# Splitting each early half gate around the values of an attention group, in a decoder step on one core

## The chip, the core and the metric

The kernel runs on one core of a Trainium2 chip. The metric is the device time of one execution in microseconds (us), and lower is better. In this text PE is the engine for matrix products (TensorE), DVE the vector engine, ACT the scalar engine, POOL the GpSimd engine, and SP the engine that issues most of the DMA transfers. PSUM is the memory that PE writes its products to, in eight banks.

## The reference

One layer of a decoder is computed for 512 prompt tokens and 8 sample tokens (520 together, D = 1024). Cut to what matters here:

```python
z = x @ w_in            # q 16x64 | k 4x64 | v 4x64 | pooling 512 | memory query 4x64 | 3 gates x 1024
o_a = sliding-window attention with sinks (window 128, blocks of 128, 16 heads)
o_b = multi-scale causal pooling, mixed and scaled
o_c = cross attention, 4 heads, 256 memory tokens
m = sigmoid(gate_0) * (o_a @ wa) + sigmoid(gate_1) * (o_b @ wb) + sigmoid(gate_2) * (o_c @ wc)
h = layer_norm(ALPHA * x + m @ w_out)
out = layer_norm(ALPHA * h + top-2 mixture of 16 SwiGLU experts(h))
```

All is float32. Products are made in float32 quality from reduced operands: each matrix is split into a high and a low part, and three products are added (high by high, low by high, high by low).

## The kernel before

There are stages on the core, one after the other: the input is transposed and projected; the keys, values and memory keys are made; then 20 attention groups run; then the branches are merged with their gates, projected and normed; and the experts come last.

The change lies in the 20 attention groups. Groups 0 to 15 are window attention ("swa": a block of 128 queries and four heads), groups 16 to 19 are memory attention. The sample tokens' own attention is cut into small steps, and one step, `sample(g)`, stands in each group. On PE a group is: transposes of the normalised probabilities (8 of them, 4 in a "narrow" group 0, 1, 8 or 9, which has one block of keys), scores of the group two ahead, values (probabilities by values), the sample step, and a "fill".

A fill is one half gate: 24 products of 260 columns that have nothing to do with the attention, for a half (260 of the 520 tokens) of one column tile of the gate weights. Fill m is half `m % 2` of gate tile `m // 2`; fills 0 to 15 are the early ones (`EARLY` = 16). Fill 0 stands ahead of the groups, group g has fill g + 1 for g up to 14, group 15 has none, and groups 16 to 19 have fills 16 to 19 with other weights. The products accumulate in PSUM bank 6, and the one after the 24th is told to ACT by `prod_ps`.

A fill waits for two things, and the engines take their instructions in the order in which they are written:

- `gate_out`: ACT has copied the half gate before it out of bank 6 (`filled`, line 790);
- `lo_split`: DVE has made the low part `flo` of the tile's weights (`gate_split`, line 1900, one subtraction of 128x1024), for which ACT first makes the high part `fhi` (line 777). A tile lasts for two fills, so a new one is needed for fills 2, 4, ..., 14, that is in groups 1, 3, ..., 13.

On DVE a group g is, in this order: the copy `pt` of half of the transposes (line 1923 or 1925), the inverse of the sums of group g + 1 (1812, 1815), a piece of the sample step, the four scaled and masked score tiles of group g + 2 (`scaled`, line 1785), the new `flo` when g is odd and under 15, the norms of the sample step, the row maximum of group g + 2 (1798, 1800), and `oalo`, the low part of the group's output (1824). On ACT it is: the exponentials of group g + 1 (695), the copy `pt` of the other half of the transposes (805), the half gate (790), `fhi` when g is odd, and `oahi` (813), the high part of the output, which waits for the values.

The fill is written after the sample step, and its waits stand at its head:

```python
last.then_inc(o_ps, 1)
sample(g)
if fill_after(g) is not None:
    fill(fill_after(g))
```

After the last early fill (`prod_ps` = 16) SP loads the first weights of the merge into the place of the gate weights, and everything later in the kernel follows on that.

Of the kernel before, what the change touches and what calls it, by code (L numbers as in the profile page):

```python
# [16 lines left out]
KD = D // P  # L17
# [40 lines left out]
def decoder_step(nc, a, o):  # L58

    ctx = ExitStack()  # L60
    with ctx:
        def sem(name):
            return ctx.enter_context(nc.semaphore(name))
# [96 lines left out]
        def rt(name, k, shape, dt=F32):  # L160
# [111 lines left out]
        prod_ps, gate_out, m_step, m_val, m_hi, m_lo = (sem(n) for n in (  # L272
            "prod_ps", "gate_out", "m_step", "m_val", "m_hi", "m_lo"))
# [36 lines left out]
        def narrow(g):  # L310

            return groups[g][0] == "swa" and groups[g][1] == 0

        def act_copies(g):

            return sum(not narrow(n) for n in range(g))
# [16 lines left out]
        EARLY = 2 * KD  # L333
        FILLS = EARLY + 4

        def fill_after(g):

            return g + 1 if g < EARLY - 1 else g if g >= EARLY else None
# [34 lines left out]
        def quarter(t, u):  # L373

            return ps[:, 4 + (2 * t + u) % 4, :].rearrange("p (k c) -> p k c", k=4)
# [673 lines left out]
        def _(pe):  # L1049
# [5 lines left out]
            for t in range(NB):  # L1055
                pe.wait_ge(x_in[t], 32 if t == NB - 1 else 16)
                for u in range(2):
# [3 lines left out]
                    for k in range(4):  # L1061
                        last = pe.transpose(quarter(t, u)[:, k, :], xtok[:, t, (4 * u + k) * P:(4 * u + k) * P + P], ident)
                    last.then_inc(xt_ps, 1)
            for k in range(KD):
                last = pe.transpose(ps[:, 3, k * NS:k * NS + NS], xsam[:, k * P:k * P + P], ident[0:NS, 0:NS])
# [15 lines left out]
            def cols(w, n):  # L1081

                return w[:, n * P:n * P + P]
# [7 lines left out]
            def xk(t, k):  # L1091
                return by_half(t[:, k * T:k * T + T])
# [20 lines left out]
            for g in range(4):  # L1113
                last = pe.transpose(ps[:, 7, g * n:g * n + n], pstate[:, g * P:g * P + P], ident[0:n, 0:n])
# [7 lines left out]
            for g in range(4):  # L1122
                for u in range(4):
                    last = pe.transpose(ps[:, 4 + g, u * P:u * P + P],
                                        mtok[:, u % 2, (2 * g + u // 2) * P:(2 * g + u // 2) * P + P], ident)
# [3 lines left out]
            for g in range(4):  # L1129
# [6 lines left out]
                for h in range(2):  # L1136
                    last = pe.matmul(ps[:, 2 * (g % 2) + h, 0:TH], wmix[:, g, :],
                                     pooled[:, g, h * TH:h * TH + TH], start=True, stop=True)
# [19 lines left out]
            for b in range(NB + 1):  # L1158
                out = ps[:, 4 + b // 2, (b % 2) * 256:(b % 2) * 256 + 256]
                last = product([out], [(xhi[:, k * T + b * P:k * T + b * P + P], xlo[:, k * T + b * P:k * T + b * P + P],  # L1160
                                        [whi[0][:, k * 256:k * 256 + 256]], [wlo[0][:, k * 256:k * 256 + 256]])
                                       for k in range(KD)])
# [8 lines left out]
            for p in range(2):  # L1171
                last = pe.transpose(ps[:, 6, p * P:p * P + P], z[:, ZK + p, SEQ - P:SEQ], ident)
            last.then_inc(row_ps, 1)
            for p in range(2):
                last = pe.transpose(ps[0:NS, 6, 256 + p * P:256 + p * P + P], z[:, ZK + p, SEQ:T], ident)
            last.then_inc(row_ps, 1)

            for g in range(4):
                last = pe.transpose(ps[0:PST + NS, 7, g * P:g * P + P], z[:, ZU + g, SEQ - PST:T], ident)
# [25 lines left out]
                pe.matmul(out, cols(wlo[s], q), mh, start=False, stop=False)  # L1205
                return pe.matmul(out, cols(whi[s], q), ml, start=False, stop=stop)  # L1206

            def fill(m):

                half = m % 2  # L1210
                if m:
                    pe.wait_ge(gate_out, m)
                else:
                    pe.wait_ge(row_out, 3)
                pe.wait_ge(lo_split, N_F + m // 2 + 1 if m < EARLY else N_G + 1)
                out = ps[:, 6, 0:TH]
                for k in range(KD):
                    mh, ml = xk(xhi, k)[half], xk(xlo, k)[half]
                    if m < EARLY:
                        pe.matmul(out, cols(fhi, k), mh, start=k == 0, stop=False)  # L1220
                        pe.matmul(out, cols(flo, k), mh, start=False, stop=False)  # L1221
                        last = pe.matmul(out, cols(fhi, k), ml, start=False, stop=k == KD - 1)  # L1222
                    else:
                        last = triple(out, A, (m - EARLY) // 2 * KD + k, mh, ml, k == 0, k == KD - 1)
                last.then_inc(prod_ps, 1)

            def merge_gates(i):
                pe.wait_ge(lo_split, 2 * i + N_G + 1)
# [43 lines left out]
            def scores(g):  # L1272
                kind, b, h = groups[g]
                if g:
                    pe.wait_ge(sc_row, g)
                if g == 2 * NB:
                    pe.wait_ge(roped, 10)
                if g == NKV * NB:
                    pe.wait_ge(mkt_out, 1)
                for j in range(2):  # L1280
                    for s in range(2):
                        rows = slice(64 * s, 64 * s + 64)
                        if kind == "swa":
                            k0, w = (0, P) if b == 0 else ((b - 1) * P, 2 * P)
                            q, k = z[rows, ZQ + 2 * h + j, b * P:b * P + P], z[rows, ZK + h // 2, k0:k0 + w]
                        else:
                            w = NMEM
                            q, k = z[rows, ZC + j, b * P:b * P + P], mkt[rows, j, :]
                        last = pe.matmul(ps[:, s, 256 * j:256 * j + w], q, k, start=True, stop=True)
                last.then_inc(sc_ps, 1)  # L1290
# [108 lines left out]
            memory(1, 1)  # L1399
            scores(1)  # L1400
            fill(0)
            for g, (kind, b, h) in enumerate(groups):
                nk = 1 if kind == "swa" and b == 0 else 2
                pe.wait_ge(sc_nrm, g + 1)
                if g:
                    if act_copies(g):
                        pe.wait_ge(pt_act, act_copies(g))
                    pe.wait_ge(pt_dve, g)
                    pe.wait_ge(o_hi, g)
                    pe.wait_ge(o_lo, g)  # L1410
                else:
                    pe.wait_ge(mkv_out, 2)
                for k in range(nk):
                    for j in range(GRP):
                        last = pe.transpose(ps[:, 4 + k, j * P:j * P + P], probs[g % 2][:, j, k * P:k * P + P], ident)
                last.then_inc(pt_ps, 1)
                if g + 2 < NGR:
                    scores(g + 2)
                if not narrow(g):
                    pe.wait_ge(pt_act, act_copies(g + 1))  # L1420
                pe.wait_ge(pt_dve, g + 1)
                if kind == "swa":
                    for k in range(nk):
                        for s in range(2):
                            c = (2 * (h // 2) + s) * HD
                            last = pe.matmul(ps[64 * s:64 * s + 64, 4, 0:2 * P], v[:, b - nk + 1 + k, c:c + HD],
                                             pt[:, k, 2 * s * P:2 * s * P + 2 * P], start=k == 0, stop=k == nk - 1)
                else:
                    for j in range(2):
                        for k in range(2):  # L1430
                            for s in range(2):
                                c = 256 + (2 * j + s) * HD
                                last = pe.matmul(ps[64 * s:64 * s + 64, 4, j * P:j * P + P], mkv[:, k, c:c + HD],
                                                 pt[:, k, (2 * s + j) * P:(2 * s + j) * P + P], start=k == 0, stop=k == 1)
                last.then_inc(o_ps, 1)
                sample(g)
                if fill_after(g) is not None:
                    fill(fill_after(g))

            pe.wait_ge(con_in, 96)  # L1440
            pe.wait_ge(sw_act, 4)
# [8 lines left out]
            for k in range(KD):  # L1450
                last = pe.matmul(ps[:, 7, 64:104].rearrange("p (u n) -> p u n", u=2), con[:, C_ONE:C_ONE + P],
                                 wgb[:, :, k, :], start=k == 0, stop=k == KD - 1)
# [90 lines left out]
            for u in range(TT):  # L1543
                last = pe.matmul(ps[0:TR, 7, (u + 1) * NE:(TT + 1) * NE].rearrange("p (t n) -> p t n", n=NE),
                                 onesb[:, :], both[:, u:u + 1, :].broadcast_to([TR, TT - u, NE]),
                                 start=False, stop=u == TT - 1, skip_group_check=True)
            last.then_inc(rank_ps, 1)

            for n in range(2 * TT):
                if n % TT == 0:  # L1550
                    pe.wait_ge(list_ok, n // TT + 1)
                last = pe.matmul(ps[:, 6, P:P + NE], rowhot[:, n // TT, n % TT, :], chunkr[:, n // TT, n % TT, :],
                                 start=n == 0, stop=n == 2 * TT - 1)
            last.then_inc(slot_ps, 1)
            pe.wait_ge(list_ok, 3)
            for n in range(2 * TT):
                last = pe.matmul(ps[:, 7, P:P + NE], rowhot[:, n // TT, n % TT, :].bitcast(F32),
                                 chunkw[:, n // TT, n % TT, :], start=n == 0, stop=n == 2 * TT - 1)
# [84 lines left out]
            with pe.If(n_over > 0):  # L1643
# [6 lines left out]
                for n in range(2 * TT):  # L1650
                    last = pe.matmul(ps[:, 7, 2 * P:2 * P + NOVER], bhot[:, n // TT, n % TT, :].bitcast(F32),
                                     bonw[:, n // TT, n % TT, :], start=n == 0, stop=n == 2 * TT - 1)
# [980 lines left out]
```

## Time and profile before

| what | value |
|---|---|
| device time, median of 3 runs | 898.4 us (896.6 to 898.66) |
| the profiled execution: its own time, its span | 900.36 us, 898.3 us |
| mean granted clock of PE | 0.957 |
| PE busy | 844.8 us (94%) |
| DVE busy | 526.4 us (59%) |
| ACT busy | 435.3 us (48%) |
| POOL busy | 165.8 us (18%) |

The profile follows one execution. A span is the time from its first to its last instruction; the execution's own time is 2.06 us longer. Busy shares are over the whole span. The granted clock is 1.00 where PE had its full 2.4 GHz, and 0.50 where it had 1.2 GHz.

### The profile page before, as it was taken

How to read it: one execution, taken by the hardware profiler on the slowest of the kernel's cores; microseconds unless marked ns; L12 is line 12 of the kernel's file. 1: busy time of each engine (PE TensorE's matmuls, PEld its weight loads, DVE VectorE, ACT ScalarE, POOL GpSimd, SP SyncE). 2: the span in 40 equal slices, each digit the busy share in tenths (PEclk: the TensorE clock that was granted, in tenths of full speed). 3: DMA queues.
4: the chain of work that ended last, by engine and by line, in shares of the span. 5: the costliest groups of instructions: out<-in, count | busy, mean ns of one | idle time of the engine just before them, and what ended most of it. 6: DMA issues, size and time to landing. Idle time of an engine off the chain costs nothing.

```text
span 898.3 us, 13926 instructions
## 1 busy us (share of the span) xinstructions
PE 844.8 (94%) x5436; PEld 745.5 (83%) x5436; DVE 526.4 (59%) x709; ACT 435.3 (48%) x578; POOL 165.8 (18%) x145
## 2 busy tenths in 40 slices
PE   8999988998997999999999998499999999999994
PEld 7999987787886989999999777387888888888882
DVE  4211155645445333444443434769999999999977
ACT  4222232555455242222222213357788778878864
POOL 0195013122222100000000055331112111211002
PEclk8999999999998699999999999589999999999997
DMA  9322200831012113222223463899999999999973
GB/s 330 117 94 93 93 25 24 301 146 48 25 48 89 47 42 131 92 88 88 88 88 115 127 203 95 289 417 403 395 400 401 386 390 401 400 385 393 399 215 95
DMA packets 38287, 179.80 MB, mean 200 GB/s; under 512 B 3935, under 2 KB 11775, under 8 KB 24126
## 3 DMA queue, kind: packets, MB, share of 16 engines
q1 hardware_dynamic: 32630, 159.22, 46.5%
q0 software_dynamic: 5600, 19.99, 8.0%
q8 instruction: 26, 0.43, 0.2%
q14 instruction: 15, 0.12, 0.0%
q10 hardware_dynamic: 16, 0.03, 0.0%
HBM read 164.65 MB, written 16.89 MB: 202 GB/s over the span
## 4 chain that ended last, share of the span: by engine, by line
PE 87%; DVE 6%; DMA 3%; issue 2%; ACT 1%; SPq 0%; DVEq 0%; POOL 0%; POOLq 0%; ACTq 0%
PE ps L1204 7%; PE ps L1205 7%; PE ps L1581 7%; PE ps L1206 7%; PE ps L1583 6%; PE ps L1582 6%; PE ps L1076 4%; PE ps L1077 4%; PE ps L1078 4%; PE ps L1608 3%; PE ps L1610 3%; PE ps L1609 3%; PE ps L1220 2%; PE ps L1222 2%; PE ps L1221 2%; PE ps L1569 2%
## 5 line engine op out<-in xcount | busy, mean ns | idle before, releaser
L2086 DVE TENSOR_TENSOR elo<-eraw,ehi 128x2048 fp32r<-128x2048 f32 x96 | 218.0, 2291 | 25.7 <-ACT ehi L899 23.7
L899 ACT ACTIVATE ehi<-eraw 128x2048 fp32r<-128x2048 f32 x96 | 183.0, 1916 | 27.2 <-PE ps L1583 16.0
L1581 PE MATMUL ps<-ehi,xethi 128*128 128x512 f32 x256 | 103.1, 403 | 3.7 <-issue 2.4
L1583 PE MATMUL ps<-elo,xethi 128*128 128x512 f32 x256 | 101.0, 395 | 0.0
L1582 PE MATMUL ps<-ehi,xetlo 128*128 128x512 f32 x256 | 101.0, 394 | 0.0
L1204 PE MATMUL ps<-xhi,whi 128*128 128x260 f32 x256 | 74.5, 291 | 0.0
L1205 PE MATMUL ps<-xhi,wlo 128*128 128x260 f32 x256 | 74.1, 290 | 0.0
L1206 PE MATMUL ps<-xlo,whi 128*128 128x260 f32 x256 | 74.0, 289 | 0.0
L1076 PE MATMUL ps<-xhi,whi 128*128 128x260 f32 x256 | 73.5, 287 | 0.0
L1077 PE MATMUL ps<-xhi,wlo 128*128 128x260 f32 x256 | 73.3, 287 | 0.0
L1078 PE MATMUL ps<-xlo,whi 128*128 128x260 f32 x256 | 73.2, 286 | 0.0
L1892 DVE TENSOR_TENSOR wlo<-late,whi 128x2048 fp32r<-128x2048 f32 (+1 forms) x16 | 34.5, 2158 | 64.4 <-ACT whi L832 64.4
L1714 DVE TENSOR_TENSOR wlo<-raw,whi 128x2048 fp32r<-128x2048 f32 x10 | 23.4, 2338 | 67.5 <-ACT whi L607 67.5
L1581 PEld LDWEIGHTS ps<-ehi,xethi 128*128 128x128 f32 x256 | 48.8, 191 | 16.7 <-DVE elo L2086 3.8
L2431 POOL TENSOR_TENSOR probs<-probs,stat 128x1024 f32<-128x1024 f32 (+1 forms) x20 | 34.4, 1722 | 128.5 <-DVE stat L1815 128.5
L1583 PEld LDWEIGHTS ps<-elo,xethi 128*128 128x128 f32 x256 | 48.6, 190 | 10.5
L1582 PEld LDWEIGHTS ps<-ehi,xetlo 128*128 128x128 f32 x256 | 48.7, 190 | 9.3
L695 ACT ACTIVATE probs<-probs,stat 128x256 f32<-128x256 f32 (+1 forms) x80 | 38.0, 476 | 36.4 <-DVE stat L1798 33.9
L1608 PE MATMUL ps<-ehi,hthi 128*128 128x512 f32 x128 | 51.3, 401 | 0.0
L2476 POOL DMA_INDIRECT f_dram<-yout,dest x14 | 28.7, 2052 | 121.4 <-ACT yout L919 121.4
L1204 PEld LDWEIGHTS ps<-xhi,whi 128*128 128x128 f32 x256 | 50.1, 196 | 0.3 <-issue 0.3
L1205 PEld LDWEIGHTS ps<-xhi,wlo 128*128 128x128 f32 x256 | 50.2, 196 | 0.0
(380 smaller groups left out, 2075.1 us busy)
## 6 DMA issues: line engine op xcount, KB each, us to landing
eraw<-w_gate_in SPq DMA_DIRECT2D x32, 1024.0 KB, 19.8
eraw<-w_up_in SPq DMA_DIRECT2D x32, 1024.0 KB, 20.3
eraw<-w_down_in SPq DMA_DIRECT2D x32, 1024.0 KB, 22.0
raw<-wz_in SPq DMA_DIRECT2D x7, 1024.0 KB, 5.2
late<-wm_in SPq DMA_DIRECT2D x8, 896.0 KB, 4.4
late<-wm_in SPq DMA_DIRECT2D x8, 704.0 KB, 4.0
fraw<-wm_in SPq DMA_DIRECT2D x8, 512.0 KB, 3.6
late<-wo_in SPq DMA_DIRECT2D x4, 1024.0 KB, 4.8
```

Source lines behind the costliest of these rows:

```text
L899: ac.activation(ehi[s % 3][:, :], eraw[s][:, :], ACT.Copy).then_inc(ehi_ok, 1)
L1076: pe.matmul(out, sh, mh[n], start=start and k == 0, stop=False)
L1077: pe.matmul(out, sl, mh[n], start=False, stop=False)
L1078: last = pe.matmul(out, sh, ml[n], start=False, stop=stop and k == len(parts) - 1)
L1204: pe.matmul(out, cols(whi[s], q), mh, start=start, stop=False)
L1205: pe.matmul(out, cols(wlo[s], q), mh, start=False, stop=False)
L1206: return pe.matmul(out, cols(whi[s], q), ml, start=False, stop=stop)
L1581: pe.matmul(ps[:, bank, :], hi[:, k, :], ehi[s[j]][:, w], start=k == 0, stop=False)
L1582: pe.matmul(ps[:, bank, :], lo[:, k, :], ehi[s[j]][:, w], start=False, stop=False)
L1583: last = pe.matmul(ps[:, bank, :], hi[:, k, :], elo[s[j]][:, w], start=False, stop=k == KD - 1)
L1608: pe.matmul(ps[:, bank + h, :], hi[:, f, :], ehi[s[j]][:, w], start=f == 0, stop=False)
L2086: ve.tensor_tensor(elo[s % 3][:, :], eraw[s][:, :], ehi[s % 3][:, :].bitcast(F32), ALU.subtract)\
```

## The change

Each early fill of the groups is written in two parts. The first 12 of its 24 products now stand between the scores and the values of the group; the other 12 stay behind the sample step. The waits at the head of `fill` are written in both parts, and the count `prod_ps` is told only after the second. Fill 0, the fills of groups 16 to 19, and the other engines' programs stay as they were.

```diff
-            def fill(m):
+            def fill(m, ks=range(KD)):
...
-                for k in range(KD):
+                for k in ks:
...
-                last.then_inc(prod_ps, 1)
+                if KD - 1 in ks:
+                    last.then_inc(prod_ps, 1)
...
                 if g + 2 < NGR:
                     scores(g + 2)
+                m = fill_after(g)
+                two = m is not None and m < EARLY
+                if two:
+                    fill(m, range(4))
                 if not narrow(g):
                     pe.wait_ge(pt_act, act_copies(g + 1))
                 pe.wait_ge(pt_dve, g + 1)
...
                 sample(g)
-                if fill_after(g) is not None:
-                    fill(fill_after(g))
+                if m is not None:
+                    fill(m, range(4, KD) if two else range(KD))
```

In group 3, an odd one, PE's order before is this. The rows are transposes (1415), scores (1289), values (1426), the sample's scores (1320) and keys (1306), and then the fill (1220 to 1222); what each waits for stands in brackets.

```order
L1415 MATMUL ps<-con,probs_92 128x128 x7
L1289 MATMUL ps<-z 128x256 [waits sc_row]
L1289 MATMUL ps<-z 128x256 x3
L1426 MATMUL ps<-pt,v 64x256 [waits pt_dve,pt_act]
L1426 MATMUL ps<-pt,v 64x256 x3
L1320 MATMUL ps<-qsp,kt 128x2x4 [waits kt_ok]
L1320 MATMUL ps<-qsp,kt 128x2x4 x3
L1306 MATMUL ps<-con,cach_k 128x128 [waits kt_ok]
L1306 MATMUL ps<-con,cach_k 128x128 x3
L1220 MATMUL ps<-xhi,fhi 128x260 [waits lo_split,gate_out]
L1221 MATMUL ps<-xhi,flo 128x260
L1222 MATMUL ps<-xlo,fhi 128x260
```

In the changed kernel the same group on PE reads as follows, from the scores (now line 1290) into the first products and, behind the twelfth, to the values (now 1431), the sample's scores (1321) and keys (1307) and the second part.

```order
L1290 MATMUL ps<-z 128x256 [waits sc_row]
L1290 MATMUL ps<-z 128x256 x3
L1220 MATMUL ps<-xhi,fhi 128x260 [waits lo_split,gate_out]
L1221 MATMUL ps<-xhi,flo 128x260
L1222 MATMUL ps<-xlo,fhi 128x260
...
L1431 MATMUL ps<-pt,v 64x256 [waits pt_dve,pt_act]
L1431 MATMUL ps<-pt,v 64x256 x3
L1321 MATMUL ps<-qsp,kt 128x2x4 [waits kt_ok]
L1321 MATMUL ps<-qsp,kt 128x2x4 x3
L1307 MATMUL ps<-con,cach_k 128x128 [waits kt_ok]
L1307 MATMUL ps<-con,cach_k 128x128 x3
L1220 MATMUL ps<-xhi,fhi 128x260 [waits lo_split,gate_out]
```

So the wait for `lo_split` and `gate_out` has moved from behind the values and the sample step to ahead of both.

On DVE nothing has moved. This is group 3 of the changed kernel, where `scaled` is line 1790 and `flo` line 1905; its first row waits for the transposes, and the row of `flo` stands behind the four score tiles, which wait for the scores (`sc_ps`).

```order
L1930 COPY pt<-ps 128x512 [waits o_ps,pt_ps]
L1817 TENSOR_TENSOR stat<-stat 128x4 [waits sc_exp]
L1820 RECIPROCAL stat<-stat 128x4 [waits sc_den]
L1790 ISA probs_92,stat<-ps,con,prm 128x256 [waits sc_ps]
L1790 ISA stat 128x1
L1790 ISA probs_92,stat<-ps,con,prm 128x256
...
L1905 TENSOR_TENSOR flo<-fraw_53,fhi 128x1024 [waits prod_ps,hi_split]
L1803 TENSOR_SCALAR stat<-stat 128x4 [waits sc_row]
L1805 TENSOR_TENSOR stat<-stat,prm 128x4 [waits sc_neg]
L1829 TENSOR_TENSOR oalo<-ps,oahi 128x2x128 [waits o_hi]
```

Only the line numbers differ from the kernel before; what moved is when PE asks for `flo`.

## Rows read from the trace of the kernel before

**Rows 1.** The page: engines' busy time, and the chain that ended last.

```profile
PE 844.8 (94%) x5436; PEld 745.5 (83%) x5436; DVE 526.4 (59%) x709; ACT 435.3 (48%) x578; POOL 165.8 (18%) x145
PE 87%; DVE 6%; DMA 3%; issue 2%; ACT 1%; SPq 0%; DVEq 0%; POOL 0%; POOLq 0%; ACTq 0%
```

**Rows 2.** Busy time by stretch, the early groups: start:end, length, engines, PEclk.

```profile
161.00:285.00 124.00, 117.53 (x929) 100.13 (x929) 64.69 (x242) 66.32 (x219) 28.77 (x17) 0.97 0.33 110
```

**Rows 3.** PE's waits from 155 to 330 us: for whom, total, times, longest.

```profile
PE ps L1220 <- DVE flo L1900: 4.4, 6, 1.8
PE ps L1426 <- DVE pt L1925: 0.5, 2, 0.2
```

**Rows 4.** Order of time on PE, group 3: start, length, what [idle before].

```profile
185.51 1.13 PE L1289 MATMUL ps<-z 64*128 64x256 f32 x8
186.58 1.08 PE L1426 MATMUL ps<-pt,v 128*64 128x256 f32 x8
187.59 1.06 PE L1320 MATMUL ps<-qsp,kt 128*128 128x8 f32 x8
188.50 0.63 PE L1306 MATMUL ps<-con,cach_k 128*128 128x128 f32 x4
189.79 0.36 PE L1220 MATMUL ps<-xhi,fhi 128*128 128x260 f32 x1 [0.66 <-DVE flo L1900]
189.99 0.28 PE L1221 MATMUL ps<-xhi,flo 128*128 128x260 f32 x1
190.11 0.28 PE L1222 MATMUL ps<-xlo,fhi 128*128 128x260 f32 x1
```

**Rows 5.** Order of time on DVE, group 3: first score tile, and flo.

```profile
186.70 0.48 DVE L1785 CUSTOM_DVE_ANT_0 probs<-ps,con,prm 128x256 f32<-128x256 f32 x1
...
188.32 1.33 DVE L1900 TENSOR_TENSOR flo<-fraw,fhi 128x1024 fp32r<-128x1024 f32 x1
```

**Rows 6.** Order of time on ACT, group 2: the half gate's copy.

```profile
178.80 0.38 ACT L790 ACTIVATE gate<-ps 128x260 f32<-128x260 f32 x1
```

**Rows 7.** PE in groups 1, 5, 9, 11, 13: first value, first product of the fill.

```profile
171.07 0.65 PE L1426 MATMUL ps<-pt,v 128*64 128x256 f32 x4
...
174.28 0.36 PE L1220 MATMUL ps<-xhi,fhi 128*128 128x260 f32 x1 [0.65 <-DVE flo L1900]
...
202.39 1.08 PE L1426 MATMUL ps<-pt,v 128*64 128x256 f32 x8
...
205.75 0.36 PE L1220 MATMUL ps<-xhi,fhi 128*128 128x260 f32 x1 [0.68 <-DVE flo L1900]
...
235.80 0.65 PE L1426 MATMUL ps<-pt,v 128*64 128x256 f32 x4
...
239.02 0.36 PE L1220 MATMUL ps<-xhi,fhi 128*128 128x260 f32 x1 [0.19 <-DVE flo L1900]
...
252.20 1.08 PE L1426 MATMUL ps<-pt,v 128*64 128x256 f32 x8
...
255.42 0.36 PE L1220 MATMUL ps<-xhi,fhi 128*128 128x260 f32 x1
...
267.32 1.08 PE L1426 MATMUL ps<-pt,v 128*64 128x256 f32 x8
...
270.54 0.36 PE L1220 MATMUL ps<-xhi,fhi 128*128 128x260 f32 x1 [1.81 <-DVE flo L1900]
```

**Rows 8.** Group 7 on PE and DVE: values, flo, the sample's transpose.

```profile
217.81 1.08 PE L1426 MATMUL ps<-pt,v 128*64 128x256 f32 x8 [0.23 <-DVE pt L1925]
...
218.93 1.23 DVE L1900 TENSOR_TENSOR flo<-fraw,fhi 128x1024 fp32r<-128x1024 f32 x1
...
221.06 0.33 PE L1349 MATMUL ps<-con,srow 128*128 128x128 f32 x1 [1.18 <-DVE sstat L1881]
```

**Rows 9.** Busy time and PEclk by stretch, around PE's slow stretches.

```profile
230.20:233.60 3.40, 3.40 (x18) 3.40 (x18) 0.00 (x0) 0.77 (x4) 0.00 (x0) 0.50 0.00 0
...
270.50:271.10 0.60, 0.56 (x5) 0.59 (x6) 0.50 (x2) 0.59 (x3) 0.00 (x0) 1.00 0.00 0
271.10:274.50 3.40, 3.40 (x19) 3.40 (x18) 0.00 (x0) 1.58 (x8) 0.00 (x0) 0.51 0.01 2
...
293.00:300.00 7.00, 7.00 (x35) 6.87 (x33) 2.96 (x4) 2.34 (x9) 0.00 (x0) 0.50 0.37 121
```

## The prediction

> **What bounds the kernel now.** I read the page first. PE is busy for 94% of the span and the chain that ended last is 87% PE, with 6% DVE [rows 1]: time that PE loses in the attention groups is lost to the end, unless something later was waiting for anything else. Then the stretch of the early groups, 161 to 285 us: PE is busy for 117.5 of 124 us at a granted clock of 0.97 [rows 2]. So there is little idle time to win there, 6.5 us at most. Then who PE waits for. The largest is the fill's first product waiting for DVE's `flo`, 4.4 us in 6 waits; the values' wait for DVE's copy of the transposes is 0.5 us in 2 [rows 3]. The place that the change fills with work, between scores and values, is therefore almost free of waiting already, and the work it moves there carries the one wait that counts.
>
> Then one odd group in order of time. In group 3 the scores run from 185.51, the values start behind them at 186.58, the sample's scores at 187.59 and keys at 188.50, and the fill's first product at 189.79, after 0.66 us idle for `flo` [rows 4]. DVE starts on the score tiles when the scores are done, at 186.70, and on `flo` at 188.32, which takes 1.33 us, to 189.65 [rows 5]; PE goes on 0.14 us later. So `flo` comes 3.21 us after the scores end (189.79 - 186.58). That is not an accident of this group: four score tiles on DVE (1.62 us) and `flo` (1.33) follow the scores, and they stay in that order in the changed kernel. Values and sample step cover 2.55 of these 3.21 us now.
>
> **The change, part by part.**
>
> *Odd groups (1, 3, ..., 13): the wait for a new `flo` moves ahead of values and sample step.* PE takes its products in order, so behind the waiting first product stand 11 products, the values, the sample step, the second part, and all later groups. PE idles from the end of the scores until `flo`, and values and sample step are run after that. What is lost in each is what covered the wait: the time from the first value to the fill's first product, less the idle time in it. From [rows 4, 7]:
>
> group 1: 174.28 - 171.07 = 3.21, less 0.65: 2.56
> group 3: 3.21 less 0.66: 2.55
> group 5: 205.75 - 202.39 = 3.36, less 0.68: 2.68
> group 9: 239.02 - 235.80 = 3.22, less 0.19: 3.03
> group 11: 255.42 - 252.20 = 3.22, no wait stood there: 3.22
> group 13: 270.54 - 267.32 = 3.22, less 1.81: 1.41
>
> Group 7 is different [rows 8]. Its scores are narrow and end 0.23 us before the values' start, at about 217.58; `flo` ends at 220.16, so with the same 0.14 PE goes on at 220.30: 2.72 us idle. Before, PE idled 0.23 for the copy and 1.18 for the sample's row, which DVE makes right behind `flo`; both vanish behind the 12 products. That leaves 2.72 - 1.41 = 1.31. The seven give 16.8 us.
>
> *Even groups (0, 2, ..., 14): `flo` is there, and only `gate_out` is new at that place.* In group 2 ACT's copy of the half gate ends at 178.80 + 0.38 = 179.18 [rows 6], and the scores, of the same length as in group 3, end later than that (the values start at 179.27). No wait; in group 6, with short scores, about 0.1. What could be won is the rest of the waits for the copies of the transposes, 0.5 us in all, of which 0.2 is already counted in group 7. I take 0.2 us won for the even groups together.
>
> *Twelve products more ahead of the values delay `o_ps`*, and with it `oahi` on ACT and `oalo` on DVE, for which the next transposes wait. Between values and transposes the second part (12 products at 0.12 us [rows 4], 1.4 us) remains, and a sample step in all but group 14. The copies need under 1 us (0.38 and 0.42 each in their rows). I cost this at nothing; were the cover gone, it would be about 1 us in a group, and it would show as the transposes waiting for `oalo`.
>
> *The cut itself.* A fill's first product takes 0.20 us to the next, against 0.12 between the others (189.79, 189.99, 190.11 [rows 4]). Now there are two such starts in a fill: 15 x 0.08 = 1.2 us. The doubled waits are already met the second time and cost nothing that a row shows. From below, this term is 0.
>
> *The clock.* It is the term of which the trace shows least. In group 13 PE idles 1.81 us; 0.56 us after it goes on, the granted clock falls from 1.00 to 0.51 for 3.4 us [rows 7, 9]. At half speed some 3.4 x (1 - 0.51) = 1.7 us of it is lost. Idles of 0.65 to 0.68 us brought no fall in the groups 1, 3 and 5, and one fall (230.2 to 233.6) came with no idle ahead of it, but behind small products of the sample step. Now seven idles of 2.7 to 3.4 us stand in the stretch, all longer than the one that the fall followed. Bounds: nothing, if the idles bring no more falls than the two of now; 7 x 1.7 = 12 us, if each brings one full slow stretch. I take 6: a fall for nearly every idle, part of each slow stretch lying in idle time or on small work, and one or two of them were there already.
>
> The Trainium skill (TensorE: Matmul & The Clock Gate, the section on HAM oscillation) says that idle gaps between bursts of products put TensorE back to half its clock, and that a loop with such a gap in each turn pays the transition in each turn. The fall in group 13 agrees; that shorter gaps did not bring one says that not every gap counts. By the rule alone the clock term would be the full 12 us.
>
> The sum is 16.8 - 0.2 + 1.2 + 6 = 23.8 us, on the profiled execution's 900.36: 924.2. The median of the runs stands 1.96 us lower, so the forecast is 898.4 + 23.8 = 922 us. The loss goes through to the end, since the merge's weights are loaded only when the last early fill is done, and PE is the bound in front of the experts.
>
> **The rivals.**
>
> *The wait, but no more slow clock than now.* All idles cost only themselves: 898.4 + 17.8 = 916. For it: idles of 0.65 us cost nothing, and a 1.18 us one in group 7 brought no fall in the next 9 us. Against it: 1.81 us was enough. I give it 0.25.
>
> *The clock falls and stays low.* From 293 to 300 us PE ran at 0.50 for 7 us on end, on small products [rows 9]. If, after each idle, values and sample step run at half clock too, some idles bring two slow stretches: nine stretches in all make 9 x 1.7 = 15 us and 898.4 + 17.8 + 15 = 931, and two for each idle 24 us and 940. I give it 0.15.
>
> *Faster: DVE's `flo` is there in time.* If the first part didn't have to wait, the 4.4 us of `flo` waits and 0.5 of copies would go: 893.5. It decides at one point: `flo` must be done when the scores end. In group 3 it would have to come 3.2 us earlier, but DVE starts it behind score tiles that need these very scores. I see no way; 0.02.
>
> *The change doesn't do what it says:* the first part runs behind the values anyway, since PE takes what is ready. Nothing in the rows shows a product passing a waiting one: in group 3 the transposes and all else stood still for the 0.66 us. The time would be 898.4. Of this, 0.02.
>
> **How the numbers follow.** Forecast with the clock term between 3 and 10 us: 0.56, 919 to 926. With the rivals at 916 (0.25) and 931 (0.15), the range that leaves out some 2 in 10 is 914 to 930; it takes in the sum without any clock term (916) and the rule's 12 us (928). A difference of 0.3% (2.7 us) is what a measurement of this kernel can tell from no change. Faster 0.02, within it 0.02, slower 0.96.
>
> **What would show it.** In the changed kernel's waits the fill's first product waits for `flo` seven times, 22 us in all (now 4.4), about 3.2 us each, standing behind the scores; no wait for `pt` ahead of values; the sample's transpose in group 7 without its 1.18 us. The even groups show no idle. The early groups, 161 to 281 us now, take some 24 us longer; the granted clock there is below 0.97, about 0.94 (6 us lost are 12 us more at half), with slow stretches soon after the idles. From the last early fill on, all lies where it lay, only later. The prediction is wrong if the waits for `flo` are short (then the DVE order was misread), if the stretch grows by 24 us and the end does not (then something later had slack), or if the clock holds.

## The result, and the profile after

The changed kernel takes 929.25 us (median of 4 runs, 925.25 to 930.93) against 898.53 us before on the same chip: a ratio of 1.0338, 95% interval 1.0304 to 1.0371. It is slower by 30.7 us, 7 us above the forecast and inside its range of 914 to 930 us by less than 1 us; two of the four runs lie above 930. Its profiled execution has a span of 928.1 us, 29.8 more than before.

These are PE's waits from 155 to 360 us in the changed kernel, the answer to [rows 3]; the columns are for whom, the total, the times, the longest:

```profile
PE ps L1220 <- DVE flo L1905: 21.7, 7, 3.3
PE ps L1438 <- DVE pt L1930: 1.8, 2, 0.9
...
PE ps L1220 <- ACT gate L790: 0.3, 1, 0.3
```

Seven waits for `flo`, 21.7 us, and the waits for `pt` ahead of the values (line 1431) and for the sample's row in group 7 are gone. Group 3 in order of time on PE and DVE, the answer to [rows 4, 5]:

```profile
190.74 1.13 PE L1290 MATMUL ps<-z 64*128 64x256 f32 x8
...
193.54 1.33 DVE L1905 TENSOR_TENSOR flo<-fraw,fhi 128x1024 fp32r<-128x1024 f32 x1
...
195.02 0.36 PE L1220 MATMUL ps<-xhi,fhi 128*128 128x260 f32 x1 [3.15 <-DVE flo L1905]
...
196.05 0.42 PE L1220 MATMUL ps<-xhi,fhi 128*128 128x260 f32 x1
196.27 0.42 PE L1221 MATMUL ps<-xhi,flo 128*128 128x260 f32 x1
...
197.48 1.77 PE L1431 MATMUL ps<-pt,v 128*64 128x256 f32 x8
199.18 1.06 PE L1321 MATMUL ps<-qsp,kt 128*128 128x8 f32 x8
200.09 0.63 PE L1307 MATMUL ps<-con,cach_k 128*128 128x128 f32 x4
200.48 0.37 PE L1220 MATMUL ps<-xhi,fhi 128*128 128x260 f32 x1
```

Scores, then 3.15 us of nothing, and only then the first products; values and sample step, which covered the wait before, come behind it. And the products start 0.12 us apart at first and 0.22 apart from 196.05 on, and the values take 1.77 us for the 1.08 of before: the clock has fallen. Busy time and PEclk of the early groups as a whole and of the slow stretches in them (start:end, length, PE, ..., PEclk third from the end):

```profile
160.00:312.10 152.10, 130.06 (x910) 108.41 (x909) 63.62 (x238) 63.09 (x212) 26.88 (x16) 0.88 0.25 84
...
175.20:182.20 7.00, 7.00 (x34) 6.02 (x34) 0.42 (x1) 3.63 (x12) 0.00 (x0) 0.53 0.88 343
195.50:199.00 3.50, 3.50 (x18) 2.52 (x17) 0.00 (x0) 0.00 (x0) 0.00 (x0) 0.51 0.00 0
216.00:219.40 3.40, 3.40 (x17) 2.03 (x15) 0.00 (x0) 0.00 (x0) 0.00 (x0) 0.50 0.48 154
246.50:250.30 3.80, 3.80 (x21) 3.47 (x20) 0.13 (x1) 1.58 (x3) 0.00 (x0) 0.55 0.00 0
253.60:267.30 13.70, 12.96 (x58) 11.67 (x60) 1.42 (x5) 3.20 (x12) 0.00 (x0) 0.50 0.13 39
280.60:284.40 3.80, 3.80 (x20) 2.43 (x19) 0.21 (x1) 0.62 (x2) 0.00 (x0) 0.55 0.00 0
301.20:305.00 3.80, 3.80 (x20) 2.37 (x20) 0.42 (x1) 1.18 (x5) 0.00 (x0) 0.55 0.01 2
```

The same stretch of work, from fill 0 to the last early fill, is this row in the kernel before:

```profile
161.00:281.10 120.10, 114.47 (x906) 98.20 (x907) 62.16 (x236) 64.03 (x212) 26.87 (x16) 0.97 0.32 106
```

It grew by 32 us. PE's idle time in it grew from 120.1 - 114.47 = 5.6 us to 152.1 - 130.06 = 22.0, by 16.4, and its busy time by 15.6 us for the same products: the first is the wait for `flo` less the small waits that went, the second the slow clock and the second start of each fill. A PEclk of 0.97 over 120.1 us is 0.03 x 120.1 / 0.5 = 7 us at half clock, two slow stretches of 3.4 us, and 0.88 over 152.1 us is 36.5 us, about eleven such lengths. The rest of the kernel took 2 us less than before in these two profiles, about what runs of one kernel differ by.

### The profile page after: what moved, and what is told of

It reads as the page before. It is cut to its first block, busy times and chain, and to the rows that moved or that the text cites. A ratio compares the mean times of both kernels' runs of the same rounds, so it can differ in the third digit from the quotient of the medians.

```text
span 928.1 us, 13941 instructions
## 1 busy us (share of the span) xinstructions
PE 860.4 (93%) x5436; PEld 755.5 (81%) x5436; DVE 526.5 (57%) x709; ACT 433.9 (47%) x578; POOL 164.4 (18%) x145
## 4 chain that ended last, share of the span: by engine, by line
PE 88%; DVE 5%; DMA 3%; issue 2%; ACT 1%; SPq 0%; DVEq 0%; POOL 0%; POOLq 0%; ACTq 0%
PE ps L1204 6%; PE ps L1205 6%; PE ps L1586 6%; PE ps L1206 6%; PE ps L1588 6%; PE ps L1587 6%; PE ps L1076 4%; PE ps L1077 4%; PE ps L1078 4%; PE ps L1613 3%; PE ps L1615 3%; PE ps L1614 3%; PE ps L1220 2%; PE ps L1431 2%; PE ps L1222 2%; PE ps L1221 2%
## 5 line engine op out<-in xcount | busy, mean ns | idle before, releaser
L1220 PE MATMUL ps<-xhi,fhi 128*128 128x260 f32 x128 | 42.0, 328 | 22.0 <-DVE flo L1905 21.7
L1586 PEld LDWEIGHTS ps<-ehi,xethi 128*128 128x128 f32 x256 | 48.8, 191 | 16.8 <-DVE elo L2091 3.8
L1615 PE MATMUL ps<-elo,hthi 128*128 128x512 f32 x128 | 49.9, 390 | 0.0
```

The lines of the kernel that those rows point to most:

```text
L1586: pe.matmul(ps[:, bank, :], hi[:, k, :], ehi[s[j]][:, w], start=k == 0, stop=False)
```

## The experiments

All runs of the kernel before that a ratio rests on were made on the same chip as the kernel compared.

**The odd groups alone.**

```diff
-                two = m is not None and m < EARLY
+                two = m is not None and m < EARLY and g % 2 == 1
```

> Only the seven fills that need a new flo (groups 1, 3, ..., 13) are cut; the even groups stand as in the kernel before. Theory (wait and slow clock of the odd groups): nearly all of the loss stays, 926 to 930 us, with seven waits for flo of about 3.1 us each. Rival (the cut and the first part ahead of the values cost something in every group): the loss is about half, 912 to 916 us.

Measured: 926.01 us, the lower edge of the expected range, ratio 1.0244 (1.0204 to 1.0284), the kernel before at 900.44 us there. The profiled execution has seven waits for `flo` with 21.7 us in all. The interval's upper end is below the lower end of the changed kernel's, so the odd groups hold most of the loss and perhaps not all; where the rest lies no run shows, since the even groups alone cost nothing (next run).

**The even groups alone.**

```diff
-                two = m is not None and m < EARLY
+                two = m is not None and m < EARLY and g % 2 == 0
```

> Only the eight fills that use a flo already made (groups 0, 2, ..., 14) are cut. Theory: the time of the kernel before, 898 to 900 us, since the restart of a fill costs 8 x 0.08 = 0.6 us and 0.2 us of waiting for the copies goes. Rival (the cut costs in every group): 910 us or more.

Measured: 898.84 us, ratio 0.9974 (0.9948 to 0.9999), as expected. The cut does no harm where `flo` is ready; eight of the fifteen cut fills cost nothing that can be measured. The rival of a cost in each group falls.

**Work in place of the idles.** The 24 added products add work and nothing to the output.

```diff
+                if two and g % 2:
+                    pe.wait_ge(gate_out, m)
+                    for n in range(24):
+                        pe.matmul(ps[:, 6, 0:TH], xhi[:, 0:P], xhi[:, 0:TH], start=True, stop=True)
                 if two:
                     fill(m, range(4))
```

> The changed kernel, with 24 products that nobody reads (260 columns each, about 2.9 us) put ahead of the wait for flo in each odd group, into the bank that the fill then overwrites. The wait for flo is as long as before, but PE works in it. Theory (the idles bring the slow clock): the clock term goes and the wait term stays, 914 to 918 us, and the slow stretches behind the waits vanish. Rival (the slow clock comes from the small products of the sample step, or from the new order, and not from the idles): 926 us or more, granted clock as in the changed kernel.

Measured: 914.92 us, in the expected range, ratio 1.0133 (1.0075 to 1.0191). Group 3 on PE, in order of time, and the busy time of all early groups:

```profile
187.58 3.12 PE L1425 MATMUL ps<-xhi 128*128 128x260 f32 x24
190.80 0.36 PE L1220 MATMUL ps<-xhi,fhi 128*128 128x260 f32 x1
...
192.39 1.08 PE L1435 MATMUL ps<-pt,v 128*64 128x256 f32 x8
```

```profile
159.00:296.30 137.30, 135.82 (x1073) 117.44 (x1074) 63.46 (x237) 62.05 (x210) 26.89 (x16) 0.99 0.27 92
```

The first product of the fill comes 3.22 us after the scores as ever (190.80 - 187.58), so the wait is whole; but the clock stays at 0.99 and the values take 1.08 us again. That separates the two terms. (In group 7 the added products run 0.6 us past `flo`, so they cost slightly more than the idle did.) With the same order and the same lateness the early groups take 137.3 us for the changed kernel's 152.1, 15 us less, and 17 us more than the 120.1 of the kernel before; by the medians the slow clock is 929.25 - 914.92 = 14 us, by the ratios (1.0338 - 1.0133) x 898.5 = 18 us (about 12 to 24 by their intervals, an estimate), and the idles' own length with the cut is what is left, 12 us by the ratio of this run (6.7 to 17 by its interval) and 17 us by the profile. The order as such, and the small products in it, bring no more slow clock than there was.

**The first part behind the values.**

```diff
-                if two:
-                    fill(m, range(4))
                 if not narrow(g):
...
                 last.then_inc(o_ps, 1)
+                if two:
+                    fill(m, range(4))
                 sample(g)
```

> The first 12 products stand behind the values and ahead of the sample step, in all early groups. The values then cover a part of the wait for flo again. Theory: the lost cover is the sample step alone, 1.98 + 1.54 + 1.67 + 0.07 + 2.45 + 2.21 + 0.40 = 10.3 us over the groups 1, 3, ..., 13, plus 1.2 us for the cut, plus 5 to 12 us of clock, since the idles are still 1.5 to 2.7 us each: 915 to 922 us. Rival (what costs is that the values come later, which holds up the copies of the output and the next transposes): 898 to 902 us.

Measured: 913.49 us, ratio 1.0115 (1.0076 to 1.0154), a little under the expected range. The waits for `flo` are 15.4 us in 8, one of them fill 0's 0.3, the longest 2.6 us, and PEclk of the early groups is 0.91:

```profile
159.00:296.10 137.10, 121.45 (x905) 105.84 (x906) 62.15 (x236) 65.30 (x211) 26.90 (x16) 0.91 0.28 93
```

The loss shrinks by more than half when the values alone cover the wait again. The rival, by which the late values were the cost, falls: here they are where they were before, and the kernel is still slower.

**`flo` two tiles earlier, in the kernel before and in the changed one.** In the odd groups:

```diff
+                        if j == 1 and f is not None:
+                            gate_split(f)
...
+                f = g // 2 + 1 if g % 2 and g < EARLY - 1 else None
                 if g + 2 < NGR:
-                    scaled(g + 2)
-                if g % 2 and g < EARLY - 1:
-                    gate_split(g // 2 + 1)
+                    scaled(g + 2, f)
```

> The kernel before, with flo made between the second and the third of the four score tiles on DVE in the odd groups, two tiles (0.8 us) earlier; the rest of DVE's work ends when it did. Theory: the waits of the uncut fill shrink by up to 0.8 us each: 0.65 + 0.66 + 0.68 + 0.19 + 0.81 = 3.0 us less, 895 to 896 us, and about 894 if the slow stretch behind group 13's wait goes too. Rival (DVE then waits for ACT's fhi, or the scores' rows come late): no change, 898 us.

> The changed kernel with the same edit on DVE. Theory: each of the seven waits falls from 3.1 to about 2.3 us, 5.6 us less in all, and the clock term stays since 2.3 us of idle is still more than the 1.81 us that brought a slow stretch in the kernel before: 922 to 925 us. Rival (the clock falls only for idles near 3 us): the clock term goes as well, 910 to 914 us.

Measured: 899.39 us with a ratio of 1.0004 (0.9987 to 1.0021) for the kernel before with this edit, and 926.29 us, ratio 1.0303 (1.0273 to 1.0334), for the changed kernel with it. Both theories failed: the waits for `flo` are still 21.6 us in 7 in the changed kernel. The first rival's "no change" came out, but not for its reasons. Group 3 of the first, on POOL, DVE and PE in order of time, shows why:

```profile
183.38 1.89 POOL L2432 TENSOR_TENSOR probs<-probs,stat 128x1024 f32<-128x1024 f32 x1 [5.42 <-DVE stat L1817]
...
183.81 0.48 DVE L1785 CUSTOM_DVE_ANT_0 probs<-ps,con,prm 128x256 f32<-128x256 f32 x1
184.22 2.14 DVE L1902 TENSOR_TENSOR flo<-fraw,fhi 128x1024 fp32r<-128x1024 f32 x1
...
186.28 0.47 DVE L1785 CUSTOM_DVE_ANT_0 probs<-ps,con,prm 128x256 f32<-128x256 f32 x1
186.50 0.36 PE L1220 MATMUL ps<-xhi,fhi 128*128 128x260 f32 x1 [0.66 <-DVE flo L1902]
```

Against the score tiles `flo` starts 0.8 us earlier, and it lasts 2.14 us for 1.33, so it ends when it did. From the end of POOL's multiplication (183.38 + 1.89 = 185.27) to its own end (184.22 + 2.14 = 186.36) are 1.09 us. It looks as if it stood still until POOL was done; the next runs test that.

**`flo` earlier and POOL's multiplication later.** POOL's multiplication waits for the inverse of the sums, which DVE makes; in the odd groups the inverse is moved behind the four tiles, beside the edit above.

```diff
-                if g + 1 < NGR:
+                if g + 1 < NGR and f is None:
                     inverse(g + 1)
...
                     scaled(g + 2, f)
+                if f is not None:
+                    inverse(g + 1)
```

> As the run in which flo was made between the second and the third score tile, in the kernel before, and in the odd groups the inverse of the sums of group g + 1 moved behind all four tiles, so that POOL's multiplication by it no longer runs while flo is made. Theory (flo took 2.14 us for 1.33 there because POOL's multiplication, started just ahead of it, held it up): flo takes about 1.1 us and comes 0.8 to 1.0 us earlier than in the kernel before; the waits for flo fall from 4.4 to about 1.5 us in all, and the time by some 3 us, to 895 or 896. Rival (the length of flo there came from its new neighbours on DVE or from ACT): flo is again 2.1 us and the time that of the kernel before.

> The same edit on DVE in the changed kernel. Theory: each of the seven waits falls from 3.1 to about 2.2 us, 15 to 16 us in all, and the time by 6 us and by what of the clock goes with it: 918 to 924 us. If the clock falls only for idles near 3 us, all of its term goes and the time is 911 to 914 us. Rival: waits of 3.1 us and 926 us, as in the run with the first edit alone.

Measured: 895.98 us, ratio 0.9962 (0.9945 to 0.9979), for the kernel before with the edit, and 916.91 us, ratio 1.0188 (1.0155 to 1.0221), for the changed kernel with it, a little under the expected 918 to 924. In the changed kernel with the edit, group 3 on DVE and PE:

```profile
187.35 1.22 DVE L1907 TENSOR_TENSOR flo<-fraw,fhi 128x1024 fp32r<-128x1024 f32 x1
...
188.72 0.36 PE L1220 MATMUL ps<-xhi,fhi 128*128 128x260 f32 x1 [2.23 <-DVE flo L1907]
```

`flo` takes 1.22 us and the wait is 2.23 for 3.15; in the seven odd groups the waits are 16.0 us for 21.7. Under 6 us less of waiting, and the kernel is 12 us faster than the changed one, so part of the clock term went too (PEclk 0.90 over 142.2 us, 28 us at half, for 36.5). Both alternatives fail, that waits of 2.2 us would keep the whole clock term and that they would lose it all: behind the waits of groups 5, 7 and 11 the clock fell, behind the other four it did not.

In the kernel before with the edit, the order of time on DVE and POOL in group 3 shows the same hold-up at another place. POOL's multiplication now starts at 186.52:

```profile
184.12 1.22 DVE L1902 TENSOR_TENSOR flo<-fraw,fhi 128x1024 fp32r<-128x1024 f32 x1
...
186.36 0.14 DVE L1800 TENSOR_SCALAR stat<-stat 128x4 f32<-128x4 f32 x1
186.52 1.89 POOL L2434 TENSOR_TENSOR probs<-probs,stat 128x1024 f32<-128x1024 f32 x1 [8.64 <-DVE stat L1817]
186.53 1.90 DVE L1802 TENSOR_TENSOR stat<-stat,prm 128x4 f32<-128x4 f32 x1
188.35 0.41 DVE L1826 TENSOR_TENSOR oalo<-ps,oahi 128x256 fp32r<-128x256 f32 x1
```

An addition of 4 columns takes 1.90 us, and the transposes then wait for `oalo`, 2.5 us in 5 waits.

**The early `flo`, and cuts in the even groups.** The edit above together with the second experiment's.

> The version that the runs point to: fills cut in the even groups alone, and flo made early and undisturbed in the odd ones. Theory: the gains add, 3 us from flo and 0 to 1 from the even groups, 894 to 896 us. Rival (nothing is won since the clock and not the waits sets what is left): 897 to 900 us.

Measured: 897.16 us, ratio 0.9984 (0.9968 to 1.0). The theory failed and the time is the rival's; whether the clock is the reason isn't shown. The gains don't add; on top of the early `flo` the cut of the even groups brings nothing.

**The inverse last.** In the odd groups of the kernel before, with `flo` early:

```diff
                     scaled(g + 2, f)
-                if f is not None:
-                    inverse(g + 1)
                 sample_norm(g)
                 if g + 2 < NGR:
                     row_max(g + 2)
+                if f is not None:
+                    inverse(g + 1)
```

> As the run before this one in the kernel before (flo between the tiles, inverse behind them), with the inverse of group g + 1 moved further back in the odd groups, behind the sample's norms and the row maximum of group g + 2. POOL's multiplication then starts behind the last DVE operation with two inputs from SBUF. Theory (POOL's multiplication holds up each such operation, whatever its size): the 1.90 us of a 4-column addition falls to 0.16, the transposes' waits for oalo fall from 2.5 to 1.4 us and the wait for the sample's row in group 7 from 2.5 to about 1.2: 893 to 895 us. Rival (POOL's result now comes too late for the next transposes): a wait for probs on POOL appears and the time is 897 us or more.

Measured: 894.64 us, ratio 0.9947 (0.9927 to 0.9968), as the theory had it and the lowest median of these runs, though its interval overlaps that of the early `flo` without this step (0.9945 to 0.9979), so the step's own gain isn't shown. DVE and POOL in an odd group, in order of time, and PE's waits in all:

```profile
188.45 0.16 DVE L1802 TENSOR_TENSOR stat<-stat,prm 128x4 f32<-128x4 f32 x1
...
188.98 1.90 POOL L2434 TENSOR_TENSOR probs<-probs,stat 128x1024 f32<-128x1024 f32 x1 [9.05 <-DVE stat L1817]
```

```profile
PE ps L1349 <- DVE sstat L1883: 1.6, 1, 1.6
PE ps L1415 <- DVE oalo L1826: 1.4, 1, 1.4
...
PE ps L1415 <- POOL probs L2434: 0.7, 3, 0.3
```

The addition takes 0.16 us again, `oalo` is waited for 1.4 us as in the kernel before, and POOL's result has become just late, 0.7 us in 3 waits; the rival's wait is there, but small. How the whole gain comes about isn't settled: the early groups of its profiled execution take 119.1 us, only 1.0 less than in the kernel before. They hold one wait of 1.08 us for a DMA (`cach_k`, at 165.25) that the profile of the kernel before has not; without it they would be some 2 us shorter, an estimate. The remaining time lay elsewhere in that execution, in 2 us less ahead of the early groups and 5 us less behind them, where the first 63.9 us had a PEclk of 0.92 for 0.84.

## Why the prediction was right

**The mechanism** was as forecast: behind the scores PE stood for `flo` in each of the seven odd groups and in no other (one wait of 0.3 us for `gate_out` is the even groups' 0.1). Forecast were 22 us of waits of about 3.2 us, measured 21.7, the longest 3.3. The order on DVE set them, as [rows 5] had it. (The 4.4 us of before had fill 0's 0.4 us in them, which is no odd group's.)

**The wait and the cut**, 16.8 - 0.2 + 1.2 = 17.8 us in the sum, measure 17 us by the profile and 12 (6.7 to 17) by the ratio of the run with work in the idles, where the clock is at least that of the kernel before. The idle time alone, forecast at 16.8 - 0.2 = 16.6 us, grew by 16.4 us in the changed kernel's profile. The rival "wait only" gave 916 us, and this run is that rival made true: 914.92.

**The delay of `o_ps`** cost nothing, as costed: the transposes wait for `oalo` once and 1.4 us, in both kernels, behind the early groups.

**The clock** is the term of the sum that was mis-sized: 6 us taken, 14 to 18 measured. Two steps of it were wrong. It was taken that a part of each slow stretch would lie in idle time, but in the changed kernel they start 0.5 to 1.3 us behind the end of a wait in five groups (in group 3 the wait ends at 195.02 and the slow stretch starts at 195.5), so all of them on work; only group 9's began in the wait. And the bound of one 3.4 us stretch for each idle, 12 us, was no bound: behind group 1's wait the clock was low for 7 us and around group 9's for 13.7, and why it stayed low there isn't shown. That was the rival "falls and stays low"; it came true in two groups. The rival's 931 us has a slip in it, since it counts nine stretches in all and takes none off for the two that were there already; but nine more is what came. The total of 36.5 us at half clock less the 7 of before is 29.5, nearly nine times 3.4, and at half speed that costs about 15 us. Only group 7's wait of 2.71 us brought no fall at once. So the time landed between the forecast's 922 and this rival's 931, nearer to the rival, which had a chance of 0.15. The way and the wait were forecast well; that the time is inside the range at all, by less than 1 us, is in part luck.

The rule of the Trainium skill (TensorE: Matmul & The Clock Gate, on HAM oscillation), that a gap in each turn of a loop costs a return to half clock in each turn, came nearer than the 6 us that I took: six of seven waits had a slow stretch at or just behind them, and with products in the gaps none had. But with `flo` early and undisturbed only three of seven such gaps had one, so not every gap pays.

**The faster rival** is refuted as a matter of size too: even with `flo` early and undisturbed, PE waits 2.2 us for it behind the scores.

## What to carry to other kernels

When independent work is moved ahead to fill a wait, its own waits move too, and on an engine that runs in order everything behind them loses its cover; read what the moved work waits for before what it may cover. An idle of PE costs its length and may cost more through the clock: here seven idles of about 3 us cost nearly as much once more; products that nobody reads, put into an idle, are a cheap way to tell the two apart. Check also which engine pair an earlier start brings together: an operation that starts sooner may only wait inside itself.

## What the runs showed of the hardware

A subtraction of 128x1024 and an addition of 128x4 on DVE, each with two inputs in SBUF, stood still while POOL's multiplication ran: `flo` took 2.14 us started 0.84 us behind POOL's, 1.33 us when only 0.24 us overlapped (in group 3 of the kernel before it started at 188.32 [rows 5], and POOL's ran from 186.67 for 1.89), and 1.22 us alone; an addition of 4 columns took 1.90 us for 0.16. The score tiles, which read PSUM, kept 0.48 us beside it, and a row maximum with one input of 128x1024 in SBUF took 1.22 us with 0.83 of it beside POOL's (at 291.94 in the kernel before) and 1.20 alone. The Trainium skill (SBUF — State Buffer, "SBUF: two separate sides") says so: the port pair that VectorE and GpSimd share is an exclusive lock, and of a vector operation with two SBUF inputs and a GpSimd operation that reads SBUF, whichever starts first holds it for its whole length while the other is fully blocked. The 1.09 us from POOL's end to the end of `flo`, nearly the 1.22 that it takes alone, agree with it.

The granted clock falls without an idle as well. In the kernel before it fell at 230.2 us [rows 9], in the changed kernel at about 246.6 and with work in all idles at 239.3, each time in group 8, behind the values of a narrow group and the products of the sample step (many of them of 8 columns and less). It isn't bound to come: with the even groups alone cut, the clock held in group 8.

Nor does the length of an idle alone say whether the clock falls. The same wait of 1.81 us in group 13 was followed by a fall in the kernel before and by none where `flo` was made two tiles earlier. With the first part behind the values, waits of 2.13 us in groups 3, 11 and 13 were followed by a fall 1.1 to 1.3 us after their ends, and waits of 2.56 us in groups 1 and 9 by none. What decides it stays open here.
